# Six subtractions of the value layer's weight split move from VectorE to GpSimd

## The reference, cut to what matters

```
xx = token_shift(x) - x
xs = x + xx * mix                      # six mixtures
r, k, v = xs[0] @ w_r, xs[1] @ w_k, xs[2] @ w_v
decay, a, g = low-rank products of xs[3..5]
kk = normalize(k * k_k);  k = k * (1 + (a - 1) * k_a)
for t in tokens, per head (16 heads of 64):
    S = S * decay_t + (S @ -kk_t) (kk_t * a_t)^T + v_t k_t^T
    y_t = S @ r_t
y = group_norm(y) ...;  return (y * g) @ w_o
```

## Time and profile before

| | us |
|---|---|
| median of three runs | 1409.09 |
| the profiled execution | 1408.4 |
| its span, first to last instruction | 1406.6 |
| PE busy | 1360.0 (97%) |
| DVE busy | 1046.8 (74%) |
| ACT busy | 734.2 (52%) |
| POOL busy | 218.9 (16%) |

### The profile page before, as it was taken

The page is one execution under the profiler, slowest core; times in us unless marked ns, Lnnn a source line. Parts: engine busy times, 40 slices in busy tenths (PEclk is TensorE's granted clock), DMA queues, the critical chain, the costliest instruction groups (busy, mean ns, idle before and its releaser), DMA issues.

```text
span 1406.6 us, 31149 instructions
## 1 busy us (share of the span) xinstructions
PE 1360.0 (97%) x12046; PEld 1297.7 (92%) x12046; DVE 1046.8 (74%) x1646; ACT 734.2 (52%) x1194; POOL 218.9 (16%) x232
## 2 busy tenths in 40 slices
PE   8999999999999999999999999999999999999997
PEld 5998899999988999999878988899999998999997
DVE  6987799988887889984686976677774557677743
ACT  4547566654556656664357543554444457544442
POOL 0000133320000223330000010113320001133300
PEclk9999999999999999999999999999999999999999
DMA  9874366798573546666431300346566443466662
GB/s 376 303 268 154 132 231 232 242 386 298 180 254 106 210 149 239 224 220 200 166 106 61 121 33 2 118 135 196 187 214 201 147 135 117 137 196 194 204 205 69
DMA packets 68440, 258.30 MB, mean 184 GB/s; under 512 B 7545, under 2 KB 9857, under 8 KB 67970
## 3 DMA queue, kind: packets, MB, share of 16 engines
q1 hardware_dynamic: 68354, 257.10, 53.3%
HBM read 256.01 MB, written 1.06 MB: 183 GB/s over the span
## 4 chain that ended last, share of the span: by engine, by line
PE 83%; DVE 11%; ACT 3%; issue 2%; DMA 1%; DVEq 0%; ACTq 0%
PE ps L742 21%; PE ps L744 21%; PE ps L743 21%; PE ps L766 3%; DVE lo L1958 2%; PE ps L703 2%; PE ps L704 1%; PE ps L705 1%; DMA modraw<-in_wmod 1%; PE ps L617 1%; DVE modraw L1964 1%; PE ps L773 1%; ACT hi L1401 1%; DVE Y L2017 1%; PE ps L1145 1%
## 5 line engine op out<-in xcount | busy, mean ns | idle before, releaser
L1958 DVE TENSOR_TENSOR lo<-raw,hi 128x1024 fp32r<-128x1024 f32 (+1 forms) x350 | 477.0, 1379 | 166.8 <-ACT hi L1401 166.0
L742 PE MATMUL ps<-OH,lo 128*128 128x256 f32 x1920 | 539.1, 281 | 5.0 <-DVE lo L1958 4.7
L743 PE MATMUL ps<-OL,hi 128*128 128x256 f32 x1920 | 532.1, 277 | 0.0
L744 PE MATMUL ps<-OH,hi 128*128 128x256 f32 x1920 | 532.1, 277 | 0.0
L1401 ACT ACTIVATE hi<-raw 128x1024 fp32r<-128x1024 f32 (+1 forms) x350 | 381.2, 1112 | 5.9 <-DVEq L2110 2.8
L742 PEld LDWEIGHTS ps<-OH,lo 128*128 128x128 f32 x1920 | 360.9, 188 | 11.9 <-DVE lo L1958 8.0
L743 PEld LDWEIGHTS ps<-OL,hi 128*128 128x128 f32 x1920 | 361.1, 188 | 0.0
L744 PEld LDWEIGHTS ps<-OH,hi 128*128 128x128 f32 x1920 | 360.9, 188 | 0.0
L742 PE MATMUL ps<-GH,lo 128*128 128x256 f32 x704 | 194.9, 277 | 0.0
L743 PE MATMUL ps<-GL,hi 128*128 128x256 f32 x704 | 194.6, 276 | 0.0
L744 PE MATMUL ps<-GH,hi 128*128 128x256 f32 x704 | 194.6, 276 | 0.0
(11 more groups left out here) (389 smaller groups left out, 2051.1 us busy)
## 6 DMA issues: line engine op xcount, KB each, us to landing
raw<-in_w SPq DMA_DIRECT2D x288, 512.0 KB, 3.9
raw<-in_w SPq DMA_DIRECT2D x64, 704.0 KB, 5.5
modraw<-in_wmod SPq DMA_DIRECT2D x71, 512.0 KB, 5.2
modlate<-in_wmod SPq DMA_DIRECT2D x10, 512.0 KB, 4.0
modlast<-in_wmod SPq DMA_DIRECT2D x7, 512.0 KB, 3.8
modfirst_a<-in_wmod SPq DMA_DIRECT2D x4, 512.0 KB, 11.6
modfirst_b<-in_wmod SPq DMA_DIRECT2D x4, 512.0 KB, 12.1
l<-in_lora_in SPq DMA_DIRECT2D x1, 1536.0 KB, 6.6
```

The costliest lines, as they stand in the source:

```text
L742: pe.matmul(bank[:, 0:T], lo[:, r, w], oh[:, k0 + k], start=first, stop=False)
L743: pe.matmul(bank[:, 0:T], hi[:, r, w], ol[:, k0 + k], start=False, stop=False)
L744: ins = pe.matmul(bank[:, 0:T], hi[:, r, w], oh[:, k0 + k], start=False, stop=final)
L1958: dve.tensor_tensor(lo[:, s, 0:kt * P], raw[:, s, 0:kt * P], hi[:, s, 0:kt * P].bitcast(F32), ALU.subtract).then_inc(lo_made, 1)
```

## The change

In DVE's program the layer `rw_v` no longer makes any `lo` of its own turns; that is units 2 to 7, six instructions. POOL makes them instead, each as one subtraction of the same size. POOL waits before each until `lo_made` says that the unit before is made (units 0 and 1 still come from DVE), so that the count stays in order, and until `hi` of the unit is made. The six stand after the setting up of `U` and ahead of the clearing of `Tm`. (The change was announced as units three to seven; the code moves six.)

```diff
@@ -1977,7 +1977,7 @@
                             ahead(i, r)
                         if evacuate and results_first:
                             evacuate(i, r, start + 4 * i + r)
-                        if isinstance(i, int) and i == 0 and r < made:
+                        if isinstance(i, int) and i == 0 and r < made or name == "rw_v":
                             pass
                         elif not (last and r >= LEAD):
                             weights_lo(name, i, r, kt)
@@ -2798,6 +2798,12 @@
             pool.wait_ge(S("u_started"), 1)
             pool.memset(U[:].rearrange("p t c -> p (t c)")[:, 0:BLK * BLK:BLK + 1], 1.0).then_inc(S("u_started"), 1)
 
+            for u in range(LEAD, COUNT["rw_v"]):
+                s = u % SLOTS
+                pool.wait_ge(lo_made, START["rw_v"] + u)
+                pool.wait_ge(hi_made, START["rw_v"] + u + 1)
+                pool.tensor_tensor(lo[:, s, 0:KT * P], raw[:, s, 0:KT * P], hi[:, s, 0:KT * P].bitcast(F32), ALU.subtract
+                                   ).then_inc(lo_made, 1)
             pool.wait_ge(S("kt_made"), 4)
             pool.memset(Tm[0:BLK, :, BLK:], 0.0).then_inc(S("zeros_made"), 1)
             pool.wait_ge(mm_done, START["rw_out"])
```

## The result

| | before | after |
|---|---|---|
| median of 20 runs, us | 1407.62 | 1411.01 |
| ratio to before, 95% interval | | 1.0027 (1.0018 to 1.0035) |
| profiled span, us | 1406.6 | 1409.1 |
| POOL busy, us | 218.9 | 231.5 |

The ratio makes +3.8 us; the forecast was +3.3. A second timing on another occasion gave 1.0030 (1.0018 to 1.0042), which makes +4.2 us.

The account below looks back on a forecast made before the run. Bound: DVE through six `lo`, then PE, with DVE's second path 1.2 us behind. Saving 6.84 against 10.5 us blocked, plus a lowered clock, gives +3.3: 1408.4 + 3.3 = 1411.7, 0.7 added for the median: 1412.4 us, range 1407.5 to 1416.0.

Parts of the forecast that it names:

- The lock: In the value layer, each POOL subtraction shuts DVE's two-SBUF-input steps out for 2.16 us; blocked in all 10.5 us.
- The deduction of 0.2 us: Per POOL subtraction, some 0.2 us of blocking falls between dependent DVE steps anyway, leaving 1.95 us for each of five.
- The first one beside the transpose: POOL's first subtraction runs beside DVE's transpose of Ld, which runs on; DVE's first step waits, costing 0.8 us.
- PE's units: PE's units of V no longer wait for DVE's low parts and end at 813.2 instead of 816.3, gaining 3.1 us.
- The wait for `kt_made` 4: PE's transposed tiles wait for this DVE result, which ended at 808.55 and was forecast at 814.5 us.
- The clock: PE idles 4.6 us ahead of the filler block; the clock probably halves, stretching the block from 2.83 to up to 5.5 us.
- the middle between 2.5 and 4.1: Delay of `first_x`: 2.5 us with the clock up, up to 4.1 with it lowered; 3.3 taken.
- Behind `first_x`: From `first_x` on, the chain through PE, DVE and ACT has no wait in which the 3.3 us shift could hide.
- sign of the opposite: The forecast fails if something behind `first_x` absorbs the delay, shown by under 580 us from there to the end.
- The steps slip between: Rival: DVE's steps slip between POOL's reads, so DVE ends 6.8 us earlier; time 1406.0 us, faster; chance 0.12.
- The clock stays up: Rival: PE's idle ahead of the filler block does not lower the clock; +2.5 us, 1411.6 us; chance 0.23.
- The lock is the whole 2.94 us: Rival: each POOL subtraction blocks DVE for 2.94 us, 14.3 us in all; +6.4 us, 1415.5 us; chance 0.10.

Follow-up runs that it names:

- experiment 1: Changed kernel with POOL's six subtractions replaced by memsets of the same tiles, writing but reading nothing: ratio 0.9977 to the kernel before.
- experiment 2: Changed kernel with POOL's six subtractions replaced by copies that read one tile instead of two: ratio 0.9987 to the kernel before.
- experiment 3: Changed kernel with the substitution's products kept in PSUM, so additions to U read one SBUF tile: none took over 0.42 us; no total time given.
- experiment 4: Kernel before with only unit 2's low part on POOL, beside DVE's transpose into Ld: U's transpose ended 0.34 us earlier; no total time given.
- before_again: The unchanged kernel before, profiled a second time: span 1403.4 us.
- experiment 5: Changed kernel with 7 filler products added on PE ahead of its wait for AR's last quarter: ratios 1.0032 and 1.0044 to the kernel before.
- e6_early: Kernel before with fewer DVE substitution steps ahead of each low part, nothing moved to POOL: ratio 1.0001 to the kernel before.
- experiment 7: The second profile of the unchanged kernel before, the same run as before_again: span 1403.4 us.

## Why the prediction was right, by its own steps

The mechanism came as forecast. That the number came so near is in part luck: two terms of the sum were some 0.8 us too small each, which makes `first_x` 1.7 us later than forecast, and what brought the time back towards the forecast is most likely a fall of the clock in the kernel before, of which the prediction did not know.

- **The lock.** Mechanism and place as forecast (experiments 1 to 4). The size was taken as 4 x 0.54 = 2.16 us, measured 2.05 to 2.22. The deduction of 0.2 us for time between dependent steps was wrong. POOL's instruction takes longer where it starts under a running step (2.57 us from 799.67, with that step until 800.00, against 2.37), so we read it that its transfer begins where a step ends and the next step waits for all of it. In all 11.3 us instead of 10.5, so DVE ended 4.5 us later instead of 3.65.
- **The first one beside the transpose**: 0.8 us forecast, 0.79 measured.
- **PE's units**: the last copy of V 3.1 us earlier, as forecast (at 27.1 us after the common point, before 30.2). The wait for `kt_made` 4, forecast at 814.5, ended at 814.7 in a profile that reaches the common point 0.6 us earlier, so at 815.3 on the forecast's scale: 0.8 late, which is the blocking that was missing above.
- **The clock**: idle of 4.6 us and the fall as forecast; the middle between 2.5 and 4.1 was too mild, the block ran wholly at the lower clock (5.49 us against the 5.5 of the bound). `first_x` was 5.0 us late, where 3.3 was forecast and 4.1 was the bound with the whole block at the lower clock; the 0.8 us of blocking that were missing make the rest.
- **Behind `first_x`** nothing of the change hides the shift. The prediction's sign of the opposite, a stretch from `first_x` to the end shorter than 580 us, did show (578.6 and 578.7 us), but `before_again` takes 578.5 as well: the 580 of the first profile had the fall of the clock in it. Up to the first copy of `Us` the change costs 3.2 to 3.4 us against the profile of before with that fall and 4.8 to 5.1 against the one without. The ratios' +3.8 and +4.2 us lie between, as they would if some executions of before have the fall; how many do is not shown. That the lock, with all that follows from it, costs the time is shown by experiments 1 and 2. The share of the lowered clock at the filler block is shown only at `first_x`, 1.5 us; the times do not show it (experiment 5).
- **The rivals.** "The steps slip between" is out: every one of POOL's six costs a step. "The clock stays up" is out: the block took 5.49 and 5.34 us in the two profiles, at a clock of 0.50 and 0.53. "The lock is the whole 2.94 us" is out: the instruction itself takes 2.37 us, and 2.05 to 2.22 are lost under it. Its source, that an instruction's fixed part grows with the columns, was the weak point. The Trainium skill's sentence (SBUF — State Buffer, section "Who interferes with whom") that the second VectorE input waits for a GpSimd read, and no memset counts, is borne out by experiments 1 and 3. That the lock lasts "for the whole instruction" (the Trainium skill, same page, section "SBUF: two separate sides") is 0.15 to 0.33 us too long here, by the two instructions of 2.37 and 2.38 us that cost 2.22 and 2.05. The estimate of 2.25 us from the Trainium skill's GPSIMD Engine Reference (section "Performance versus the Vector engine") was near the 2.37 us measured for the shortest of the six.

## What to carry to other kernels

Before giving POOL an elementwise piece of DVE's work, look at what DVE does meanwhile: beside steps that read two tiles of SBUF, POOL's piece cost DVE nearly its whole length (2.05 to 2.2 us here), which is more than DVE needed to do it (1.14). It was free here only beside instructions with at most one input in SBUF, or where DVE had slack above it. And when two engines' ends lie 1.2 us apart, moving one alone gains 1.2 us at most: reorder both.

## What the runs showed of the hardware that was not expected

- POOL's copy of one tile locks too: DVE lost 0.7 to 0.9 us under copies of 1.04 to 1.39.
- The clock can stay low through a stretch in which PE's timeline is full. In the profile of `e6_early` it fell at 826.4 us, after a stretch with PE busy 2.40 of 3.40 us, and stayed at 0.50 for 17 us, in which PE ran 310 products on 32 or 64 rows and six on 128:

```profile
823.00:826.40 3.40, 2.40 (x86) 1.68 (x86) 3.37 (x3) 1.65 (x2) 0.00 (x0) 1.00 0.00 0
826.40:843.40 17.00, 17.00 (x316) 14.29 (x311) 5.83 (x10) 6.12 (x9) 0.00 (x0) 0.50 0.01 3
```

  In `before_again` the products of the same lines ran at 1.00 (experiment 7). The stretch from `first_x` to the first copy of `Us` took 31.2 us in that execution of `e6_early` instead of 22.1, and its time was 1413.74 us, where the median of the twelve is 1406.25. Time and mean clock go together in these twelve, from 1402.58 us at 0.998 to this one at 0.988.
